# Who asks for x and for the small vectors at the head of a one-core decoder layer

## The reference, cut to what matters

```
c_act = silu(c)
sh1, sc1, gt1, ... sh3, sc3, gt3 = split(c_act @ w_ada + b_ada)      # nine vectors of 1024
h = rmsnorm(x, g_ffn1) * (1 + sc1) + sh1
x = x + 0.5 * (1 + gt1) * SwiGLU_1(h)
h = rmsnorm(x, g_mix) * (1 + sc2) + sh2
x = x + (1 + gt2) * Mix(h)          # two attention branches, gated and merged
h = rmsnorm(x, g_ffn2) * (1 + sc3) + sh3
x = x + 0.5 * (1 + gt3) * SwiGLU_2(h)
out = rmsnorm(x, g_final)
```

## Time and profile before

| | us |
|---|---|
| median of 3 runs (1207.38 to 1208.82) | 1208.52 |
| the profiled execution, its own time | 1206.98 |
| its span, first to last instruction | 1205.1 |
| PE busy | 1164.1 (97%) |
| DVE / ACT / POOL busy | 578.6 / 407.8 / 308.4 |

### The profile page before, as it was taken

How to read it: one execution, slowest core, us unless ns; L and a number is a source line. 1 busy time by engine, 2 the same in 40 slices (tenths; PEclk the granted TensorE clock), 3 DMA queues, 4 the chain that set the end, 5 groups by cost and what they waited for, 6 DMA issues and landing times.

```text
span 1205.1 us, 14862 instructions
## 1 busy us (share of the span) xinstructions
PE 1164.1 (97%) x5459; PEld 916.5 (76%) x5459; DVE 578.6 (48%) x831; ACT 407.8 (34%) x636; POOL 308.4 (26%) x238
## 2 busy tenths in 40 slices
PE   6899999998999999999999999999999999999997
PEld 2588888887888878667666667887888888888885
DVE  4644444444344252579987665646333333332331
ACT  3433333332122232133544555424232232322223
POOL 0399999999974010000000000000000000000000
PEclk9999999999999999999999999999999999999999
DMA  9675574565543224212121112221324233242221
GB/s 337 175 222 163 168 225 156 167 228 175 195 153 111 72 54 130 71 35 71 53 54 45 50 47 88 88 75 48 122 70 131 78 93 116 70 135 93 86 70 70
DMA packets 156857, 138.22 MB, mean 115 GB/s; under 512 B 3359, under 2 KB 151186, under 8 KB 156818
## 3 DMA queue, kind: packets, MB, share of 16 engines
q1 hardware_dynamic: 127668, 108.33, 28.9%
q10 hardware_dynamic: 29150, 29.37, 7.6%
HBM read 135.59 MB, written 2.10 MB: 114 GB/s over the span
## 4 chain that ended last, share of the span: by engine, by line
PE 61%; POOL 16%; issue 10%; DVE 8%; ACT 4%; POOLq 1%; ACTq 0%; DVEq 0%
PE ps L345 18%; PE ps L347 18%; PE ps L346 18%; POOL ada L1337 9%; POOL ada L1333 7%; DVE prob L1252 2%; DVE nmax L1255 2%; ACT prob L1035 1%; PE ps L906 1%; DVE score L1219 1%; ACT probT L1044 1%; PE ps L881 1%; DVE max L1217 1%; PE ps L891 1%; ACT w_hi L322 1%
## 5 line engine op out<-in xcount | busy, mean ns | idle before, releaser
L327 DVE TENSOR_TENSOR w_lo<-raw,w_hi 128x1024 fp32r<-128x1024 f32 (+1 forms) x168 | 243.7, 1451 | 438.1 <-ACT w_hi L322 438.1
L345 PE MATMUL ps<-h_hi,w_hi 128*128 128x512 f32 x1024 | 412.6, 403 | 6.1 <-DVE h_lo L433 3.2
L347 PE MATMUL ps<-h_hi,w_lo 128*128 128x512 f32 x1024 | 400.6, 391 | 0.0
L346 PE MATMUL ps<-h_lo,w_hi 128*128 128x512 f32 x1024 | 400.5, 391 | 0.0
L322 ACT ACTIVATE w_hi<-raw 128x1024 fp32r<-128x1024 f32 (+1 forms) x168 | 187.6, 1117 | 318.3 <-PE ps L347 317.7
L345 PEld LDWEIGHTS ps<-h_hi,w_hi 128*128 128x128 f32 x1024 | 193.3, 189 | 62.3 <-issue 15.1
L347 PEld LDWEIGHTS ps<-h_hi,w_lo 128*128 128x128 f32 x1024 | 192.9, 188 | 41.0
L346 PEld LDWEIGHTS ps<-h_lo,w_hi 128*128 128x128 f32 x1024 | 193.4, 189 | 36.4 <-issue 0.5
L1337 POOL TENSOR_TENSOR ada<-ada 128x512 f32<-128x512 f32 x112 | 142.5, 1273 | 8.8
L345 PE MATMUL ps<-g_hi,w_hi 128*128 128x512 f32 x352 | 140.1, 398 | 0.0
L346 PE MATMUL ps<-g_lo,w_hi 128*128 128x512 f32 x352 | 138.1, 392 | 0.0
(11 more groups left out here) (163 smaller groups left out, 885.4 us busy)
## 6 DMA issues: line engine op xcount, KB each, us to landing
raw<-in_w_ffn SPq DMA_DIRECT2D x42, 1024.0 KB, 5.4
ada<-in_w_ada ACTq DMA_DIRECT2D x28, 1024.0 KB, 6.5
raw<-in_w_ffn SPq DMA_DIRECT2D x16, 1408.0 KB, 6.2
raw<-in_w_in SPq DMA_DIRECT2D x64, 256.0 KB, 3.2
ada<-in_w_ada SPq DMA_DIRECT2D x8, 1024.0 KB, 14.3
raw<-in_w_out SPq DMA_DIRECT2D x16, 256.0 KB, 3.0
x_tok<-in_x SPq DMA_DIRECT2D x4, 512.0 KB, 5.3
raw<-in_w_ffn SPq DMA_DIRECT2D x4, 512.0 KB, 10.8
```

The source lines that it names most:

```text
L327: nc.vector.tensor_tensor(tiles_of(w_lo[j % SPL], nk), raw_of(f, j, nk), tiles_of(w_hi[j % SPL], nk).bitcast(F32), ALU.subtract).then_inc( ...
L345: nc.tensor.matmul(ps[:, bank, :], hi, rhs_hi, start=start, stop=False)
L346: nc.tensor.matmul(ps[:, bank, :], hi, rhs_lo, start=False, stop=False)
L347: return nc.tensor.matmul(ps[:, bank, :], lo, rhs_hi, start=False, stop=stop)
```

## The change

The five small transfers that SP asked for first are taken from SP's list and put at the head of ACT's. Nothing else is changed: the same twelve small transfers, the same semaphore, the same sizes.

```
         @block.sync
         def _(sp):
-            load_rows(sp, ((R_C, c_in), (R_BADA, b_ada), (R_G1, g_ffn1), (R_GM, g_mix), (R_G2, g_ffn2)))
             for t in range(QT):
                 sp.dma_start(x_tok[:, t, :], x_in[0, t * P:(t + 1) * P, :]).then_inc(x_in_done[t], 16)
...
         @block.scalar
         def _(act):
+            load_rows(act, ((R_C, c_in), (R_BADA, b_ada), (R_G1, g_ffn1), (R_GM, g_mix), (R_G2, g_ffn2)))
             load_rows(act, ((R_CQ, g_cq), (R_CKV, g_ckv)))
```

## The result

| | before | after |
|---|---|---|
| median of 7 runs each, us | 1208.56 | 1212.6 |
| all runs, lowest to highest | 1206.6 to 1210.53 | 1208.5 to 1214.14 |
| the profiled execution, its own time | 1206.98 | 1208.50 |
| its span | 1205.1 | 1206.7 |

The ratio after to before is 1.0032, with a 95% interval from 1.0016 to 1.0048: the changed kernel is slower, by 1.9 to 5.8 us.

What follows compares the result with a forecast made beforehand. The head was taken to bound the kernel, paced by DVE's last odd copy of xT at 17.03 us. Late vectors 4.6 plus PE's clock 1.0 gave 5.6 us later, 1214.1 us on the median; 8-in-10 range 1209.6 to 1219.3.

Steps and rivals of the forecast that it cites:

- r: Moment PE gets the small vectors, the last of twelve having landed; 6.00 us before, forecast 12.3.
- r + 7.3: When PE can start tile k = 4, after ACT's squares, square root table and first even copy; 15.0 us before.
- from there on the two traces should run in parallel: From PE's first unit on, forecast at 48.9 us instead of 43.25, the head's shift stays unchanged to the end.
- my own sign: The prediction would be wrong if a shift of the head didn't reach the end of the program.
- PE's transposes should not start before 10 us: Sign in the head: an earlier start of PE's transposes would show the forecast wrong; rows were due at 12.3.
- the fourth step: Small transfers beside x wait behind some 1,000 packets already taken in: r = 12.3, head 4.6 us later.
- The rival that counted the stock in bytes: Vectors wait behind 1.0 MB already taken in, 2.6 us: r = 8.8, head 1.1 later, 1209.9 us; chance 0.10.
- the fifth step: PE's clock falls while it stands before k = 4; 1.0 us counted of a possible 1.6 for the last 16 transposes.
- the case to which I gave 0.62: The forecast itself: r from 10.9 without the clock's part to 14 with all of it, 1211.7 to 1216.4 us.
- nothing waits: Rival: small transfers slip between the large ones as if alone; r = 7.7, d = 0, 1208.5 us; chance 0.10.
- strict order of asking: Rival: everything asked for before 4.7 us goes first, including w_ada's third piece; r = 17.4, 1219.2 us; chance 0.13.
- one turn each: Rival: every small transfer waits for one whole transfer of q1, until 31 us; d is 23, 1232 us; chance 0.05.

Runs made afterwards that it cites:

- again: The changed kernel once more, unaltered, for a second trace; 1213.15 us, ratio 1.0036 to the kernel before.
- x, then vectors, on SP: Kernel before, with SP asking for x first, then its five small vectors, then w_ada; ACT asks for its seven as before; 1213.3 us, ratio 1.0034.
- w_ada after the vectors: Changed kernel, but SP asks for w_ada only when all small vectors have landed, x still first; 1212.72 us, ratio 1.0036.
- four on SP: Changed kernel with the four shortest small transfers (g_kidx, b_kidx, twice each) on SP ahead of x, the other eight on ACT; 1208.57 us, ratio 0.9994.
- 16 idle calls: Changed kernel with 16 idle matmul calls on PE between the transposes of k = 3 and k = 4; 1211.63 us, ratio 1.0023.
- 50 idle calls: Changed kernel with ACT's squares ahead of c_act and 50 idle matmul calls on PE ahead of the vectors' transposes; 1209.11 us, ratio 1.0006.
- moving the squares: Changed kernel with ACT's four squares of x ahead of c_act, silu table loaded before them; 1207.98 us, ratio 0.9984.

## Why the prediction was right, and which step was mis-sized

Right: the direction, the reason and the place. 1212.6 us lies within 1209.6 to 1219.3 and 1.5 under the 1214.1. The head followed DVE's last odd copy, and that followed ACT's first even copy, which hangs on r. "r + 7.3" for the start of k = 4 held in every trace in which ACT kept its order and r was the limit:

| kernel | r | r + 7.3 | start of k = 4 | first unit |
|---|---|---|---|---|
| changed | 9.74 | 17.04 | 17.06 | 46.79 |
| again | 9.70 | 17.00 | 17.02 | 46.81 |
| x, then vectors, on SP | 9.71 | 17.01 | 17.03 | 46.58 |
| w_ada after the vectors | 8.97 | 16.27 | 16.29 | 46.22 |
| four on SP | 8.34 | 15.64 | 15.66 | 44.56 |
| 16 idle calls | 9.99 | 17.29 | 17.32 | 45.55 |

Right only in the main: that the time follows the head. Of the seven kernels timed with a head 2.3 to 3.5 us later (the changed one twice) six are slower beyond noise, all but the one with 50 idle calls, and moving the squares takes that away. But the four short vectors on SP (head +1.3 us, time at most +0.6) don't show it, and in both traces of the changed kernel the shift of the head doesn't reach the end as it was (1.5 and -1.3 us of 3.5). That "from there on the two traces should run in parallel" was wrong, and by my own sign that case spoke against the forecast. So did another: PE's transposes should not start before 10 us, and those of the vectors start at 9.74, those of x at 9.99.

Right too: x lands in time and PE waits for the vectors instead, and ACT's squares follow each other without a gap. That moving the squares ahead takes the loss away, with r unchanged at 9.77, shows that the late vectors cost through ACT's order.

Mis-sized, the fourth step: r was put at 12.3 and measured 9.74 and 9.70, so that this term was 2.1 us and not 4.6. I had taken the wait of a large transfer at 287 us, counted it in packets, and let w_ada's packets stand in that stock. With w_ada held back r is still 8.97, so x makes about four fifths of the wait or more, and the packet count was the wrong measure. The rival that counted the stock in bytes came nearer: 8.8 against 9.74, and for "four on SP", with its last request at 3.47, by the same sum 3.47 + 0.95 + 2.6 + 0.55 = 7.6 against 8.34. It falls short by 0.9 and 0.8 us, so it isn't shown either. What exactly the two queues do with many small transfers beside a large one stays open.

Mis-sized, the fifth step: the clock cost 1.5 us, of a possible 1.6, where I counted 1.0. With the idle matmuls before them the same 16 transposes took 1.97 us, which showed it to be the clock.

Sum: 2.06 + 1.5 = 3.5 us in the head, forecast 5.6; the medians differ by 4.0 us, with an interval of 1.9 to 5.8. The two errors partly made up for each other, the first being the larger. There is luck in the number: the case to which I gave 0.62 had r from 10.9 to 14, which was not met; its times began at 1211.7, and without the clock 2.06 us would have given 1210.6. The clock's larger part brought the time in.

The other rivals: that nothing waits (r = 7.7) is refuted by r = 9.7 in two traces; strict order of asking (17.4) and one turn each (31) by the same number. The round-robin rule of the Trainium skill's page "DMA: Bandwidth & Descriptors", section "Queues, rings and completion order", lets a DMA engine drain a whole packet of at most 64 descriptors before it goes to the next queue. Turns of a whole large transfer for each small one would have given the 31 us, and the trace doesn't show them; with smaller turns the rule doesn't contradict 53 packets of q10 beside 265 of q1.

## What to carry to other kernels

Look for what the first instruction of each engine's chain waits for, and ask for that first: here 60 KB of small vectors that gate silu, squares and copies were worth more than the 2 MB of x that gate PE's transposes. A small transfer asked for beside large ones isn't small in time (here the vectors were there 4.5 us after the end of their last request, and 1.0 with nothing beside them); it was so behind x on the same queue and beside it on the other. And where an early transfer is to pay, the in-order engine behind it must be able to use it: the same change of the requests gave +3.5 us in the head with the squares behind c_act and -0.7 with them ahead.

## What the runs showed of the hardware that I had not expected

Twelve small requests from one engine, with nothing beside them, are served by 5.90 us; five and seven from two engines, with x asked for from 2.67 us on beside the last of them, by 6.00. So the one longer list cost no more than x beside the two shorter ones.

PE's wait for POOL near 299 us is 3.6 us in ten traces and under 0.6 in three, and its granted clock dips for some microseconds in some executions and not in others (1.00, 0.58 and 1.00 over the same 8 us at 726, in the trace of before and the two of the changed kernel). Each of these moves the time of a 1.2 ms kernel by some 3 us. Heads that differ by 2 us were at the edge of what 6 to 12 timed runs could tell apart.
